# A weight load that waits for less: w_down of the first expert asked for at the gather's issue

## The chip, the cores and the metric

The kernel runs on one core of one Trainium2 chip. The metric is the device time of one launch in microseconds (us); times before and after are medians of several runs. Five engines work beside each other from queues of their own: TensorE (PE; its weight loads are PEld), VectorE (DVE), ScalarE (ACT), GpSimd (POOL) and SyncE (SP), which here only issues transfers. "SPq" and "POOLq" are the sequencers of SyncE and GpSimd. The transfers of all of them run on 16 DMA engines. Engines wait for each other through semaphores.

## The reference, cut to what matters

One layer of a hybrid encoder over 512 tokens of width 1024. First come differential attention and a state-space mixer (some 830 us of the span, not touched here); then the mixture of experts around whose start the change lies; then a gated per-layer embedding and a last norm.

```
h2 = rms_norm(x)                                   # 512 x 1024
logits = h2 @ router_w + router_b                  # 32 experts
top-4 experts for each token, softmax gates
for each expert e, on the rows of h2 that chose it:
    gu = x_e @ w_up[e] + b_up[e]                   # 1024 -> 2048
    act = (clip(u) + 1) * g * sigmoid(1.702 g)
    out = act @ w_down[e] + b_down[e]              # 1024 -> 1024
x += sum over each token's four outs, by gate
x += sigmoid(rms_norm(x) @ w_ple_gate) * (p @ w_ple_proj)
y = rms_norm(x)
```

## The kernel before

Each expert is a block of 96 rows (CAP). The rows of a block are gathered from h2_dram by GpSimd (`fetch`, an indirect DMA with a list of token numbers) into the tile xg; TensorE turns them in eight transposes (`turn_x`), VectorE copies the result out of PSUM (`copy_x`, L1864), and TensorE multiplies them by w_up (`up`, 192 matmuls of 512 columns and 12 for the bias, L2017). ScalarE and VectorE make the activation, TensorE turns it (`turn_act`) and multiplies it by w_down (`down`, 144 matmuls) one round later. So a round is: `up(b)`, `turn_x(b + 1)`, `down(b - 1)`, `turn_act(b)`. In rounds 3, 7, 11, ... a block is small and takes less of TensorE. With these inputs no expert needs a second block.

The weights of an expert are 8 MB of w_up and 4 MB of w_down. The on-chip memory holds one expert's w_up, in eight tiles of 1 MB, and one expert's w_down, in four pairs of 1 MB. SyncE asks for each tile of the next expert as soon as TensorE has used that tile for the last time (`up_used`, `down_used`). All of SyncE's transfers stand in one queue of the DMA engines, q1, in the order in which they were asked for; GpSimd's gathers are in q0, ScalarE's stores in q10.

Before the first expert the order is written out by hand (L578 to L600). SyncE loads w_up of expert 0 early, then four rows of w_ple_gate, then the biases of expert 0 once the routing is chosen (L590 to L592). Then it waits until the rows of the first gather have landed (`xg_landed`, L593) and asks for w_down of expert 0 (L594, issued at L569), then for the other rows of w_ple_gate when TensorE has finished the projections (`ple_projected`, L595), then for w_up of expert 1, tile by tile as TensorE frees them (L598, issued at L555). w_down of expert 0 is wanted by TensorE only in round 1, after `up(1)`.

GpSimd waits for the table of slots (`tables_ready`) and for h2 to be stored, and issues gather 0 (`fetch(0)`). `fetch(1)` waits for its landing and for the transposes of block 0 (`x_turned`), since both gathers write xg. `gather_cleared` is incremented ahead of each gather at L741; nothing in the kernel before waits for it. VectorE, meanwhile, works on the tables for the later blocks (L1820 to L1859) and comes to `copy_x(0)` behind them.

Of the kernel before, what the change touches and what calls it, by code (L numbers as in the profile page):

```python
# [119 lines left out]
def wait(eng, sem, value):  # L120

    if not isinstance(value, int) or value > 0:
        eng.wait_ge(sem, value)
# [30 lines left out]
def build(nc, x, p, mix_norm_w, w_in, lambda_q1, lambda_k1, lambda_q2, lambda_k2, da_head_norm_w,  # L154
# [3 lines left out]
    with ExitStack() as ctx:  # L158
# [3 lines left out]
        def sem(name):  # L162
            return ctx.enter_context(nc.semaphore(name))
# [285 lines left out]
        rstd_ready, gather_cleared = sem("rstd_ready"), sem("gather_cleared")  # L449
# [35 lines left out]
        def _(sp):  # L485
# [79 lines left out]
            def load_down(i, expert):  # L565
                for c in range(KT // 2):
                    if not isinstance(i, int) or i:
                        sp.wait_ge(down_used, KT * (i - 1) + 2 * c + 2)
                    sp.dma_start(w_dn_pair[c], w_dn_d[ds(expert, 1), c].rearrange("e p a n -> (e p) a n")  # L569
                                 ).then_inc(rows_landed[c], 16)  # L570

            def load_bias_down(i, expert):
                wait(sp, down_done, i)
                for n in range(2):
                    sp.dma_start(bias_dn[32 * n:32 * n + 3, 0:D - 512 * n],  # L575
                                 bdn_dram[:, ds(expert * D + n * 512, D - 512 * n)]).then_inc(bias_dn_landed, 16)
# [13 lines left out]
            sp.wait_ge(chosen_ready, TT)  # L590
            load_bias_up(0, 0)
            load_bias_down(0, 0)  # L592
            sp.wait_ge(xg_landed, 16)  # L593
            load_down(0, 0)  # L594
            sp.wait_ge(ple_projected, 2 * TT)  # L595
            for k in range(4, KT):
# [61 lines left out]
        def _(pool):  # L658
# [69 lines left out]
            def fetch(b, column=None):  # L728

                wait(pool, xg_landed, 16 * b)  # L730
                if isinstance(b, int) and b < 2:
                    wait(pool, x_turned, b)
                    token = slot_token[:, b:b + 1]
                else:
                    if column is None:
                        column = pool.value_load(control[0:1, ds(b, 1)], min_val=0, max_val=BLOCKS - 1)
                    pool.tensor_copy(block_token[:], slot_token[:, ds(column, 1)]).then_inc(block_token_ready, 1)
                    pool.wait_ge(block_token_ready, b - 1)
                    wait(pool, x_turned, b)
                    token = block_token[:]  # L740
                pool.sem_inc(gather_cleared, 1)  # L741
                pool.indirect_dma_start(xg, None, h2_dram, bass.IndirectOffsetOnAxis(token, 0), bounds_check=SEQ - 1,  # L742
                                        oob_is_err=False).then_inc(xg_landed, 16)

            def experts_again():
                with pool.Fori(EXPERTS, ROUNDS) as b:
                    fetch(b, pool.value_load(control[0:1, ds(b + AGAIN, 1)], min_val=0, max_val=BLOCKS - 1))

            pool.wait_ge(tables_ready, 1)
            for b in range(2):  # L750
                pool.wait_ge(h2_stored[b], 16 * TT // 2)
            fetch(0)
            fetch(1)
            pool.wait_ge(tables_ready, 3)
            with pool.Fori(2, EXPERTS) as b:
# [1912 lines left out]
```

## Time and profile before

| what | us |
|---|---|
| median of 3 runs | 1959.93 (1958.43 to 1961.11) |
| the profiled execution | 1959.75 |
| its span in the trace | 1958.0 |
| TensorE busy in the span | 1889.7 (97%) |
| VectorE / ScalarE / GpSimd busy | 709.3 / 482.6 / 101.8 |
| DMA, mean over the span | 261 GB/s, 511.92 MB |

Times in the rows are microseconds from the start of the span unless marked ns. In windows, each engine's busy time stands with its number of instructions, then PEclk, the clock of TensorE that was granted as a share of full speed, the busy share of the 16 DMA engines, and GB/s. The share comes out slightly over 1 when they are all busy. In a row of a line, the durations are min/median/max in ns, and then come the first and last start. In a row of a queue stand packets, MB and the share of the 16 engines' time. A row of landing gives the time from a transfer's issue until its semaphore said that it was complete, min/median/max.

### The profile page before, as it was taken

The page shows a single profiled execution, that of the slowest core. Times are in us where ns is not written, and L with a number is a line of the kernel's source. Part 1 is how long each engine was busy: PE and PEld are TensorE (multiplying, and loading weights), DVE is VectorE, ACT ScalarE, POOL GpSimd, SP SyncE. Part 2 cuts the span into 40 slices and gives each one's busy share as a digit, 9 for nine tenths or more (in the row PEclk, how much of TensorE's full clock was granted, in tenths as well). Part 3 has the DMA queues.
Part 4 walks back from the last instruction along what each step waited for, and adds up shares of the span by engine and source line. Part 5 has one row for each costly group of instructions (what it writes and reads, how often), then busy time and mean ns, then how long its engine had stood idle before and what let it go on. Part 6 is the DMA issues. An engine that isn't in the chain of part 4 may idle for free.

```text
span 1958.0 us, 37027 instructions
## 1 busy us (share of the span) xinstructions
PE 1889.7 (97%) x15105; PEld 1115.0 (57%) x15105; DVE 709.3 (36%) x1104; ACT 482.6 (25%) x736; POOL 101.8 (5%) x137
## 2 busy tenths in 40 slices
PE   6999999999999999989999999999999999999998
PEld 4777788888888888833434334343333343433346
DVE  5666768887865445261001010010100000101056
ACT  3444443535435333211000110001010000010135
POOL 2000001001020000000000000000000000000030
PEclk8999999999999999999999999999999999999999
DMA  4333322222222543299999999999999999999962
GB/s 129 88 89 106 85 76 65 67 73 64 65 64 66 150 117 98 102 377 415 407 415 417 415 415 414 414 412 412 410 414 411 408 413 414 407 411 405 408 243 94
DMA packets 206279, 511.92 MB, mean 261 GB/s; under 512 B 16341, under 2 KB 127558, under 8 KB 173382
## 3 DMA queue, kind: packets, MB, share of 16 engines
q1 hardware_dynamic: 189296, 474.68, 63.3%
q10 hardware_dynamic: 9942, 18.50, 2.8%
q0 software_dynamic: 6912, 16.79, 2.4%
q8 instruction: 110, 1.80, 0.4%
q14 instruction: 19, 0.16, 0.0%
HBM read 497.79 MB, written 20.51 MB: 265 GB/s over the span
## 4 chain that ended last, share of the span: by engine, by line
PE 69%; SPq 15%; DMA 7%; DVE 4%; issue 2%; ACT 2%; ACTq 0%; POOL 0%; DVEq 0%
PE psum L2017 65%; SPq L569 7%; DMA arena<-bup_dram 7%; SPq L555 3%; SPq L562 3%; SPq L575 2%; PE psum L2408 1%; PE psum L2416 1%; DVE arena L1436 1%; SPq L603 0%; PE psum L2079 0%; DMA arena<-y_dram,rows_u 0%; PE psum L2187 0%; PE psum L2147 0%; ACT w_hi L816 0%
## 5 line engine op out<-in xcount | busy, mean ns | idle before, releaser
L2017 PE MATMUL psum<-arena 128*32 128x512 f32 (+5 forms) x10352 | 1054.3, 529 | 30.8 <-DMA arena<-in_w_up 9.3
L2017 PEld LDWEIGHTS psum<-arena 128*32 128x32 f32 (+2 forms) x10352 | 434.0, 115 | 604.3 <-issue 423.2
L1870 DVE TENSOR_SCALAR arena<-psum 128x768 f32<-128x768 f32 (+1 forms) x32 | 28.8, 899 | 921.2 <-ACT arena L1141 921.2
L2017 PE MATMUL psum<-h_hi,w_hi 128*128 128x512 f32 x640 | 258.7, 404 | 1.3 <-DVE w_lo L1320 1.3
L2017 PE MATMUL psum<-h_hi,w_lo 128*128 128x512 f32 x640 | 249.9, 390 | 0.0
L2017 PE MATMUL psum<-h_lo,w_hi 128*128 128x512 f32 x640 | 249.4, 390 | 0.0
L1320 DVE TENSOR_TENSOR w_lo<-arena,w_hi 128x1024 fp32r<-128x1024 f32 x104 | 135.7, 1305 | 187.5 <-ACT w_hi L816 186.6
L1141 ACT ACTIVATE arena<-psum 128x768 f32<-128x768 f32 (+1 forms) x32 | 24.5, 764 | 570.5 <-PE psum L2017 570.5
L2017 PEld LDWEIGHTS psum<-h_hi,w_hi 128*128 128x128 f32 x640 | 120.3, 188 | 34.5 <-issue 8.8
L2017 PEld LDWEIGHTS psum<-h_lo,w_hi 128*128 128x128 f32 x640 | 120.4, 188 | 26.4 <-issue 2.9
L2017 PEld LDWEIGHTS psum<-h_hi,w_lo 128*128 128x128 f32 x640 | 120.1, 188 | 25.8
L816 ACT ACTIVATE w_hi<-arena 128x1024 fp32r<-128x1024 f32 x104 | 109.6, 1055 | 96.1 <-PE psum L2017 96.1
L1167 ACT ACTIVATE arena<-psum 128x768 f32<-128x768 f32 (+1 forms) x32 | 24.5, 764 | 336.6 <-PE psum L2416 336.6
L742 POOL DMA_INDIRECT arena<-h_dram,block_token x30 | 30.7, 1022 | 657.0 <-PE psum L2408 657.0
L890 ACT ACTIVATE arena<-psum 128x512 f32<-128x512 f32 x40 | 23.8, 596 | 149.6 <-PE psum L2017 149.5
L708 POOL TENSOR_TENSOR arena<-after,gdta 128x1024 f32<-128x1024 f32 x16 | 33.0, 2064 | 511.0 <-DVE gdta L1519 371.0
L1504 DVE SCALAR_TENSOR_TENSOR arena<-arena,gconv 128x512 f32<-128x512 f32 x72 | 54.2, 752 | 2.6
L2017 PE MATMUL psum<-ys_hi,w_hi 128*128 128x512 f32 x128 | 49.8, 389 | 0.0
L2017 PE MATMUL psum<-ys_lo,w_hi 128*128 128x512 f32 x128 | 49.8, 389 | 0.0
L2017 PE MATMUL psum<-ys_hi,w_lo 128*128 128x512 f32 x128 | 49.8, 389 | 0.0
L870 ACT ACTIVATE arena<-arena,small 128x128 f32<-128x128 f32 (+3 forms) x64 | 35.5, 555 | 31.1 <-DVE small L1442 31.1
L2017 PEld LDWEIGHTS psum<-arena,ones_bf 32*32 32x32 bf16 (+1 forms) x609 | 8.2, 88 | 45.3 <-issue 43.4
(381 smaller groups left out, 1627.8 us busy)
## 6 DMA issues: line engine op xcount, KB each, us to landing
arena<-in_w_up SPq DMA_DIRECT2D x256, 1024.0 KB, 18.7
arena<-in_w_down SPq DMA_DIRECT2D x128, 1024.0 KB, 22.7
arena<-in_w_in SPq DMA_DIRECT2D x80, 512.0 KB, 3.9
arena<-in_w_ssd_branch SPq DMA_DIRECT2D x16, 512.0 KB, 4.1
y_dram<-arena ACTq DMA_DIRECT2D x24, 288.0 KB, 6.6
y_dram<-arena ACTq DMA_DIRECT2D x8, 512.0 KB, 4.0
arena<-in_w_attn_branch SPq DMA_DIRECT2D x8, 512.0 KB, 3.9
arena<-in_w_out SPq DMA_DIRECT2D x8, 512.0 KB, 4.6
```

Source lines behind the costliest of these rows:

```text
L555: sp.dma_start(w_up_part[k], w_up_d[ds(expert, 1), k].rearrange("a p n -> (a p) n")).then_inc(w_up_landed[k], 16)
L562: sp.dma_start(bias_up[32 * r:32 * r + 3, :].rearrange("q (c n) -> q c n", c=2), rows[:, r:STRIPS + 1:STRIPS - r]).then_inc(bias_up_landed ...
L569: sp.dma_start(w_dn_pair[c], w_dn_d[ds(expert, 1), c].rearrange("e p a n -> (e p) a n")).then_inc(rows_landed[c], 16)
L575: sp.dma_start(bias_dn[32 * n:32 * n + 3, 0:D - 512 * n], bdn_dram[:, ds(expert * D + n * 512, D - 512 * n)]).then_inc(bias_dn_landed, 16)
L708: pool.tensor_tensor(dta_after, after[:].unsqueeze(1).broadcast_to([P, HG, P]), gdta[:, c, :].unsqueeze(2).broadcast_to([P, HG, P]), ALU.m ...
L742: pool.indirect_dma_start(xg, None, h2_dram, bass.IndirectOffsetOnAxis(token, 0), bounds_check=SEQ - 1, oob_is_err=False).then_inc(xg_land ...
L816: act.activation(w_hi[:, unit.slot], w_raw[unit.slot], ACT.Copy).then_inc(hi_ready, 1)
L870: ins = act.activation(s, s, ACT.Exp, bias=amax[:, 2 * q + m:2 * q + m + 1], accum_out=asum[:, 2 * q + m:2 * q + m + 1])
L1320: dve.tensor_tensor(w_lo[:, unit.slot], w_raw[unit.slot], w_hi[:, unit.slot].bitcast(F32), ALU.subtract).then_inc(lo_ready, 1)
L1504: ins = dve.scalar_tensor_tensor(out=o, in0=r[:, k:k + SEQ], scalar=gconv[:, k, i:i + 1], in1=o, op0=ALU.mult, op1=ALU.add)
L1870: dve.tensor_scalar(u_sb[:, 0:n], up_psum[:, 0:n, 1, :], 1.0 + LIMIT, 1.0 - LIMIT, ALU.min, ALU.max).then_inc(u_ready, 1)
L2017: return pe.matmul(o, l, r, start=start, stop=stop)
```

## The change

SyncE's wait ahead of the first w_down is for `gather_cleared` at 2 instead of `xg_landed` at 16. `gather_cleared` reaches 1 ahead of the first gather, as before, and 2 by a new increment that GpSimd executes behind it, in block 0 alone. Nothing else is changed; the gather still lands in xg, TensorE still waits for `xg_landed`.

```
@@ block.sync
             load_bias_up(0, 0)
             load_bias_down(0, 0)
-            sp.wait_ge(xg_landed, 16)
+            sp.wait_ge(gather_cleared, 2)
             load_down(0, 0)
             sp.wait_ge(ple_projected, 2 * TT)
@@ block.gpsimd, fetch(b)
                 pool.sem_inc(gather_cleared, 1)
                 pool.indirect_dma_start(xg, None, h2_dram, bass.IndirectOffsetOnAxis(token, 0), bounds_check=SEQ - 1,
                                         oob_is_err=False).then_inc(xg_landed, 16)
+                if isinstance(b, int) and b == 0:
+                    pool.sem_inc(gather_cleared, 1)
```

## Rows read from the trace of the kernel before

**Rows 1.** The page: busy time, GB/s in 40 slices, chain by engine

```profile
PE 1889.7 (97%) x15105; PEld 1115.0 (57%) x15105; DVE 709.3 (36%) x1104; ACT 482.6 (25%) x736; POOL 101.8 (5%) x137
...
GB/s 129 88 89 106 85 76 65 67 73 64 65 64 66 150 117 98 102 377 415 407 415 417 415 415 414 414 412 412 410 414 411 408 413 414 407 411 405 408 243 94
...
PE 69%; SPq 15%; DMA 7%; DVE 4%; issue 2%; ACT 2%; ACTq 0%; POOL 0%; DVEq 0%
```

**Rows 2.** Two long windows; columns: stretch, length, busy by engine, PEclk, DMA share, GB/s

```profile
860.00:1240.00 380.00, 377.32 (x4031) 151.08 (x4035) 38.67 (x58) 34.36 (x46) 14.64 (x25) 1.00 1.02 414
1240.00:1840.00 600.00, 581.11 (x6153) 227.86 (x6149) 48.93 (x57) 51.54 (x68) 21.50 (x35) 1.00 1.01 411
```

**Rows 3.** TensorE's largest wait for a transfer after 960 (us in total, times, longest)

```profile
PE psum L2017 <- DMA arena<-in_w_up: 9.3, 13, 1.2
```

**Rows 4.** Windows around the first gather, columns as in rows 2

```profile
854.00:859.00 5.00, 3.15 (x12) 1.30 (x11) 3.79 (x17) 1.20 (x3) 0.87 (x2) 0.90 0.51 121
857.00:858.00 1.00, 0.87 (x8) 0.69 (x8) 0.83 (x6) 0.00 (x0) 0.00 (x0) 1.00 0.00 0
```

**Rows 5.** Timelines of SP, POOL, PE and DVE, 840 to 910 (start, length, both us)

```profile
856.98 2.13 SPq L569 DMA_DIRECT2D arena<-in_w_down  x4
859.16 2.02 SPq L597 DMA_DIRECT2D pg_raw<-in_w_ple_gate  x4
...
853.45 1.24 POOL L742 DMA_INDIRECT arena<-h_dram,slot_token  x1 [72.81 <-DVE control L1828]
...
851.89 4.38 PE L2017 MATMUL psum<-w_pp,p_turned_at 128*128 128x512 f32 x6
857.09 0.87 PE L2408 MATMUL psum<-ident,arena 96*128 96x96 f32 x8 [0.81 <-DMA arena<-h_dram,slot_token]
860.14 20.81 PE L2017 MATMUL psum<-arena 128*32 128x512 f32 x192 [2.19 <-DVE arena L1864]
...
885.08 0.94 PE L2416 MATMUL psum<-ident,arena 128*128 128x128 f32 x6 [2.53 <-DVE arena L1878]
885.95 22.38 PE L2017 MATMUL psum<-arena 128*32 128x512 f32 x192
...
859.13 0.96 DVE L1864 COPY arena<-psum 128x768 f32<-128x768 f32 x1 [0.97 <-DVE rows_u L1859]
```

**Rows 6.** GpSimd at the third gather: its sequencer (POOLq) and the gather, by line

```profile
L742 POOLq MOVE  x1: 38/38/38, 882.2 to 882.2; - x1
L742 POOL DMA_INDIRECT arena<-h_dram,block_token x1: 1025/1025/1025, 883.0 to 883.0; - x1
...
L755 POOLq ALU_OP  x1: 38/38/38, 882.8 to 882.8; - x1
```

**Rows 7.** Gathers to landing: first, second, other 30; queues in 860:863, in 863:865

```profile
DMA to landing us min/median/max: 3.5/3.5/3.5
...
DMA to landing us min/median/max: 8.0/8.0/8.0
...
DMA to landing us min/median/max: 7.1/8.6/9.5
...
q1 hardware_dynamic: 321, 1.25, 102.1%
...
q0 software_dynamic: 123, 0.31, 40.0%
```

**Rows 8.** Window in TensorE's second expert, matmuls and weight loads alone, PEclk, DMA share, GB/s

```profile
886.00:890.60 4.60, 4.60 (x32) 1.12 (x36) 0.65 1.03 419
```

**Rows 9.** Requests of 1 MB issued at 857.0, 890.5, 946.0, to landing; gather queue in 948:950

```profile
DMA to landing us min/median/max: 4.9/4.9/4.9
...
DMA to landing us min/median/max: 9.2/9.2/9.2
...
DMA to landing us min/median/max: 7.6/7.6/7.6
...
q0 software_dynamic: 105, 0.18, 24.6%
```

More of the change, by code:

```diff
@@ L592, in _ @@
             load_bias_down(0, 0)
-            sp.wait_ge(xg_landed, 16)
+            sp.wait_ge(gather_cleared, 2)
             load_down(0, 0)
@@ L743, in fetch @@
                                         oob_is_err=False).then_inc(xg_landed, 16)
+                if isinstance(b, int) and b == 0:
+                    pool.sem_inc(gather_cleared, 1)
             def experts_again():
```

## The prediction

> **What bounds the kernel now.** I read the page first. TensorE is busy 97% of the span, and the chain that ended last is 69% TensorE, 15% SyncE's issuing and 7% transfers. The GB/s row is between 64 and 150 in the first 17 slices and above 400 in almost all of the expert stage [rows 1]. So that stage may be bound by transfers, by TensorE, or by each in turn. Two long windows tell which: from 860 to 1240 and from 1240 to 1840 the DMA engines have no idle time (share 1.02 and 1.01, 414 and 411 GB/s), and TensorE is idle for 2.7 us of the first 380 and 18.9 us of the next 600 [rows 2]. The 2.7 us is a wait for VectorE of 2.53 [rows 5]; later it waits for transfers, the weights of w_up above all (9.3 us in 13 waits) [rows 3]. So TensorE catches up with a stream of transfers that never pauses, and the place of the last bytes in that stream sets the end.
>
> From this follows the accounting. A transfer asked for earlier helps if the stream had a hole that it fills, and if no later hole opens for it. A later TensorE hurts only if it frees a weight buffer so late that the stream runs dry.
>
> There is a hole. From 854 to 859 the traffic is 121 GB/s on the mean, with none at 857 [rows 4]. The timelines around it [rows 5]: GpSimd's first gather is recorded at 853.45 for 1.24 us. SyncE asks for w_down at 856.98, when that gather has landed. TensorE turns the gathered rows at 857.09 to 857.96, VectorE, busy with the routing tables until then, copies them at 859.13, and TensorE starts the first expert at 860.14.
>
> **The change, step by step.**
>
> *When SyncE wakes.* The new increment stands behind the gather in GpSimd's program. It fires either when the sequencer comes to it or when the list is written. Behind the third gather the sequencer starts the loop's next instruction at 882.8, while the gather is recorded at 883.0 and lasts 1.02 us more: it doesn't wait for the list [rows 6]. By this spacing the increment comes 0.2 us ahead of the first gather's record, at about 853.2; if it waits for the list, at 853.45 + 1.24 = 854.7. The request for w_down moves forward from 856.98 by 3.8 us, or else by 2.3. I take the first.
>
> The Trainium skill (Perfetto Trace Analysis, DMA Instruction — SWDGE and Sequencer-only Instruction) has the sequencer ready for its next instruction as soon as the gather is pushed into the wait queue, and an instruction of the sequencer alone executed there. This agrees with the row of the third gather, and speaks against the change: the wait would then hold w_down back for nothing that the gather has done.
>
> *SyncE's queue behind it.* The four w_down requests take 2.13 us of issuing. The four rows of w_ple_gate behind them wait for TensorE's projections, which end at 851.89 + 4.38 = 856.3, so they issue from 856.3 instead of 859.16 [rows 5]. The next request, w_up of expert 1, waits for TensorE's first freed buffer and follows TensorE. On GpSimd's queue the second gather waits for the first one's rows and their transposes; it moves with them, and is wanted only after the first expert, 21 us on.
>
> *What the gather pays.* Before, the stream was running out as the first gather was issued, and it landed in 3.5 us. The second, issued among the requests for w_down and w_ple_gate, took 8.0; the other 30 took 7.1 to 9.5 [rows 7]. With w_down asked for at 853.2, the first is in the place of the second: requests of 1 MB are in the queue when its list is complete. I take 8.0, which is 4.5 us later. Bounds: 3.6 (7.1), 6.0 (9.5), and 0 if its packets still go first (rival 1). The transposes then end at 857.96 + 4.5 = 862.5.
>
> Some of this is hidden. VectorE takes the turned rows at 859.13 whatever comes before, 1.1 us after it could have had them (857.96 and the 0.1 of a hand-over). So TensorE's first expert starts 4.5 − 1.1 = 3.4 us later, near 863.5 (bounds 2.5 to 4.9). All of TensorE up to 1240 follows, since it waits for no transfer there [rows 2].
>
> *How two queues share.* From 860 to 863, 1.2 to 4.2 us into the second gather, the only queue of the DMA engines at work is SyncE's, q1, at 102.1%; from 863 to 865 the gather's queue q0 has 40% of their time for 0.31 MB [rows 7]. So the sharing itself is mild, and most of the price is that the gather's first packets move late. The Trainium skill (DMA: Bandwidth & Descriptors, Queues, rings and completion order) says that each DMA engine takes turns between its queues, packet by packet. The row of 863 to 865 agrees; by that rule alone the gather would lose only about the time of its own bytes, and the change would end as rival 1 does. The row of 860 to 863 is against it.
>
> *The clock.* After the idle of 2.53 us before 885.08, the granted clock of 886 to 890.6 is 0.65, a mixture of TensorE's two levels of 1.2 and 2.4 GHz, and the 192 matmuls there take 22.38 us against 20.81 in the first expert [rows 5, 8]. Now TensorE is to do only 0.87 us of transposes from 856.3 to 863.5. The price is between 0 and 22.38 − 20.81 = 1.6 us; I take the middle, 0.8. TensorE is then 3.4 + 0.8 = 4.2 us late.
>
> *What a late TensorE costs.* How near the stream is to running dry can be read from the weight requests, which SyncE makes when TensorE frees a buffer. Into the empty queue at 857.0 a request of 1 MB landed in 4.9 us. At 890.5 it took 9.2 us, and the shortest in that stretch, at 946.0, took 7.6 [rows 9]; so the stream had at most 7.6 − 4.9 = 2.7 us of earlier work before it. Part of this isn't cover but sharing with the gather of that time, which moved 0.18 MB in 948 to 950 and a little before; 0.3 MB at 414 GB/s is 0.7 us. I take 2.0 us of cover, near the upper bound since only the gather speaks against that; bounds 2.7, and 0 if all of the difference is sharing and late completion.
>
> *The sum.* A stream that runs dry at 946 starts again at TensorE's pace, and what was gained at 855 comes out there as a hole. So the end moves by TensorE's delay less the cover: 4.5 − 1.1 + 0.8 − 2.0 = +2.2 us. With the cheap bounds of all it is 3.6 − 1.1 + 0 − 2.7 = −0.2, with the dear ones 6.0 − 1.1 + 1.6 − 0 = +6.5. The profiled execution took 1959.75 us around its span of 1958.0, the median of the three runs is 1959.93; I put the shift on the median: 1962.1. Costed at nothing: the increment itself, on a sequencer that then waits for the landing anyway, and VectorE's work behind the copy, which moves 3.4 us and isn't wanted during the 20.81 us of the first expert.
>
> **The rivals.**
>
> *1. The gather isn't slowed*, because the increment waits for the list or the gather's packets move ahead of w_down's. For it: the gather would have a start of about a microsecond, and the sharing is mild. Against: all 31 gathers in a busy stream took 7.1 us or more. TensorE then keeps its times, and the stream moves forward by no more than the cover at 946: −2.0 us, 1957.9 (1957.2 with 2.7, 1960 with none).
>
> *2. No cover at 946* (the other side, slower by over 0.2%). The 7.6 us there are sharing and late completion, and nothing is queued when the request comes. For it: it is the shortest landing of the stage. Against: the DMA share has no gap, here or anywhere [rows 2]. The whole delay of 4.2 us comes out: 1964.1. It decides from a cover below 0.3 us.
>
> *3. The full hole is gained.* TensorE's delay never empties the stream, as it catches up by 1240 anyhow. The five microseconds lack 5 × (414 − 121) / 414 = 3.5 us of traffic; the gather's late bytes need some of it, so some 3 us are gained: 1956.9. Against: the shortness of the 7.6.
>
> **How the numbers follow.** Forecast 0.50, rival 1 0.22, rival 2 0.18, rival 3 0.10. What a measurement of this kernel can tell from no change is about 0.2%, 3.9 us. The forecast's own range is 1960 to 1965.5, of which I put 0.07 above +3.9 us; of rival 2, whose price is 0.3 above that bound, 0.12. Below −3.9 us lie 0.03 of rival 3 and 0.02 of rival 1. So slower 0.19, faster 0.05, the same 0.76. The range that leaves out no more than 0.2 goes from the low end of rival 1 to the forecast's upper end: 1957.2 to 1965.5.
>
> **What would show it.** SyncE's w_down request at 853.2 (854.7 by the other reading). No microsecond without traffic at 855 to 859. The first gather landing in 8.0 us, TensorE's first expert at 863.5, perhaps with a lower clock behind it. A DMA share below 1 near 950. From then on the same pace as before, everything 2 us later. The prediction is wrong if the first gather lands in under 5 us, if no hole opens near 950, or if TensorE's delay leaves no trace at the end.

## The result

The changed kernel takes 1965.05 us (median of 10, 1963.99 to 1967.12), the kernel before 1959.74 us (median of 10, 1958.43 to 1961.69): the ratio is 1.0027 with a 95% interval of 1.0018 to 1.0036, so +5.3 us, slower by over 0.2%. The forecast was 1962.1 in a range of 1957.2 to 1965.5. Its mechanism holds in the main: the gather is slowed, TensorE is late, and the stream of transfers runs dry for it. The hole came at another place than forecast, and the price was under-estimated by 3 us.

The profiled execution took 1965.11 us around a span of 1963.4. Times of two executions are compared from the start of the first gather's record: 853.45 before [rows 5], 852.27 now. Nothing ahead of it was changed in any kernel here, and yet it starts between 851.83 and 854.13 in the 13 profiled executions. First come the timelines of the changed kernel that answer to [rows 5] (start, length):

Timeline, the changed kernel:

```profile
852.06 2.12 SPq L569 DMA_DIRECT2D arena<-in_w_down  x4
855.14 1.82 SPq L597 DMA_DIRECT2D pg_raw<-in_w_ple_gate  x4
...
852.27 1.24 POOL L742 DMA_INDIRECT arena<-h_dram,slot_token  x1 [72.81 <-DVE control L1830]
...
860.43 1.54 PE L2410 MATMUL psum<-ident,arena 96*128 96x96 f32 x8 [5.33 <-DMA arena<-h_dram,slot_token]
863.02 23.03 PE L2019 MATMUL psum<-arena 128*32 128x512 f32 x192 [1.05 <-DVE arena L1866]
...
890.18 0.87 PE L2418 MATMUL psum<-ident,arena 128*128 128x128 f32 x6 [2.53 <-DVE arena L1880]
890.99 22.50 PE L2019 MATMUL psum<-arena 128*32 128x512 f32 x192
...
862.01 0.96 DVE L1866 COPY arena<-psum 128x768 f32<-128x768 f32 x1 [5.04 <-PE psum L2410]
```

By line, the changed kernel:

```profile
L745 POOLq EVENT_SEMAPHORE  x1: 17/17/17, 852.0 to 852.0; - x1
```

The new increment (L745) runs at 852.0, ahead of the gather's record at 852.27 that it stands behind in the program, and SyncE's w_down request follows at 852.06. So it was the sequencer's, as forecast; the request comes 0.2 us before the gather's record instead of 3.5 us after it. TensorE gets the rows at 860.43 after 5.33 us of waiting, runs the transposes in 1.54 us instead of 0.87, and begins the first expert at 863.02: 10.75 us after the gather's record, where it was 6.69. From the gather's record to the end of the span it is 1963.4 − 852.27 = 1111.1 us, where it was 1958.0 − 853.45 = 1104.6.

How the gather landed, and the queues up to its first packets (853.5 to 856.75) and from there (856.75 to 860), answering to [rows 7]:

By line, the changed kernel:

```profile
DMA to landing us min/median/max: 8.1/8.1/8.1
```

DMA queues, the changed kernel:

```profile
q1 hardware_dynamic: 302, 1.17, 89.8%
...
q1 hardware_dynamic: 285, 1.10, 82.7%
q0 software_dynamic: 144, 0.25, 20.1%
```

The gather lands in 8.1 us instead of 3.5. Its list is complete at 852.27 + 1.24 = 853.5, and for 3.2 us the only queue that moves anything is SyncE's; the gather's 0.25 MB come after 856.75, among w_down's. In the kernel before its first packets moved at 855.3, some 0.6 us after its list was complete at 854.7. So 2.6 of the 4.6 us are a later start, and the other 2.0 us come while the two queues share the engines. The windows that answer to [rows 2, 4] follow, with 858 to 859 (TensorE waits), 863 to 867 (the first expert), 890 to 900 and 950 to 960 added:

Windows, the changed kernel:

```profile
854.00:859.00 5.00, 1.11 (x3) 0.19 (x1) 2.77 (x12) 1.81 (x2) 0.00 (x0) 0.83 1.02 414
858.00:859.00 1.00, 0.00 (x0) 0.00 (x0) 0.00 (x0) 1.00 (x1) 0.00 (x0) 0.50 1.00 406
863.00:867.00 4.00, 3.98 (x20) 0.97 (x24) 3.93 (x18) 0.00 (x0) 0.84 (x1) 0.50 1.04 412
890.00:900.00 10.00, 9.82 (x74) 3.23 (x78) 0.13 (x1) 0.81 (x1) 0.18 (x1) 0.83 0.51 181
950.00:960.00 10.00, 10.00 (x144) 6.21 (x137) 1.08 (x2) 0.13 (x1) 0.24 (x2) 1.00 1.00 377
1240.00:1840.00 600.00, 581.51 (x6142) 227.44 (x6138) 46.52 (x55) 51.52 (x68) 21.55 (x35) 1.00 1.01 411
```

The hole at 854 to 859 is gone: 414 GB/s instead of 121. The clock is at 0.50, the lower level of 1.2 GHz, from 858 on, while TensorE waits, and the first expert runs at it until past 867. The hole comes back at 890 to 900, where the DMA engines are busy for 0.51 of the time at 181 GB/s: half of ten microseconds is lost where 3.5 were gained. Near 950, where it was forecast, there is none (the share is 1.01 in 940 to 950 and 1.00 in 950 to 960). From 1240 the stream is as full as before (1.01, 411 GB/s), so nothing makes up for it.

The Trainium skill (Perfetto Trace Analysis, Sequencer-only Instruction) says that the profiled window of such an instruction is its execution by the sequencer; L745's 17 ns at 852.0, before the gather's record has begun, agree with that.

### The profile page after: what moved, and what is told of

Read it like the earlier page. It is cut to its first block, busy times and chain, and to the rows that moved or that the text cites. A ratio compares the mean times of both kernels' runs of the same rounds, so it can differ in the third digit from the quotient of the medians.

```text
span 1963.4 us, 37028 instructions
## 1 busy us (share of the span) xinstructions
PE 1892.6 (96%) x15105; PEld 1117.9 (57%) x15105; DVE 709.3 (36%) x1104; ACT 482.6 (25%) x736; POOL 103.1 (5%) x137
## 4 chain that ended last, share of the span: by engine, by line
PE 70%; SPq 12%; DMA 11%; DVE 4%; issue 2%; ACT 2%; ACTq 0%; DVEq 0%; POOLq 0%
PE psum L2019 66%; DMA arena<-bup_dram 10%; SPq L569 5%; SPq L555 3%; SPq L562 2%; SPq L575 1%; PE psum L2410 1%; DVE arena L1438 1%; PE psum L2418 1%; PE psum L2081 0%; DMA arena<-h_dram,slot_token 0%; PE psum L2189 0%; SPq L603 0%; PE psum L2149 0%; ACT w_hi L818 0%
```

## The experiments

Theory A: the gather pays for the w_down requests that are queued when its list is complete; TensorE's lateness, with a share for its clock, empties the stream later on; the filled hole is worth nothing by itself. Rivals: B, any w_down beside the gather slows it; and, of the end, that w_down's early transfers cost something by themselves.

In the table, "TensorE" is the start of the third expert's w_up product counted from the first gather's record, in the profiled execution, against 921.06 − 853.45 = 67.61 us of the kernel before (line below). The end is the ratio to the kernel before, run on the same chip. Each median is of 8 to 11 runs.

The third expert, the kernel before and the changed kernel:

```profile
921.06 9.22 PE L2017 MATMUL psum<-arena 128*32 128x512 f32 x84
...
926.23 4.07 PE L2019 MATMUL psum<-arena 128*32 128x512 f32 x36
```

| kernel | gather lands | TensorE, us against before | median, us | ratio (95% interval) |
|---|---|---|---|---|
| changed kernel | 8.1 | +6.4 | 1965.05 | 1.0027 (1.0018 to 1.0036) |
| changed kernel again | 8.0 | +6.1 | 1965.44 | 1.0027 (1.0016 to 1.0037) |
| 1: request behind the written list | 3.6 | 0.0 | 1959.99 | 1.0001 (0.9992 to 1.0010) |
| 2: 1 MB of w_down early | 5.3 | +3.1 | 1962.29 | 1.0018 (1.0009 to 1.0027) |
| 3: request 3 us later than before | 3.6 | +0.1 | 1962.04 | 1.0014 (1.0005 to 1.0023) |
| 4: TensorE held back | 3.6 | +6.2 | 1963.78 | 1.0021 (1.0012 to 1.0030) |
| 5: change, TensorE kept busy | 8.0 | +2.0 | 1960.53 | 1.0006 (0.9997 to 1.0016) |
| 6: before, second wait filled | 3.6 | +1.2 | 1960.00 | 1.0003 (0.9994 to 1.0012) |
| 7: 1 and 6 together | 3.6 | −1.7 | 1957.15 | 0.9990 (0.9981 to 0.9999) |
| 8: before, both waits filled | 3.7 | −0.4 | 1960.01 | 1.0003 (0.9994 to 1.0012) |
| 9: 1 and 8 together | 3.6 | −1.7 | 1957.59 | 0.9985 (0.9976 to 0.9994) |
| 1 again | 3.6 | 0.0 | 1959.76 | 0.9999 (0.9989 to 1.0008) |

The profiled executions also have an end of their own, counted from the gather's record to the end of the span, against the 1104.6 us of before: +6.6 and +6.1 in the changed kernel, +5.4 in experiment 4, +2.6 in 2, +2.3 in 5, +3.1 in 3, −0.7 and −0.2 in 1. So TensorE's lateness comes out nearly whole where it is late. Single executions are rough: experiments 7 and 9, both 1.7 us early, are at −3.1 and −0.8.

**1. The increment behind the written list.**

```
-                    pool.sem_inc(gather_cleared, 1)
+                    own.then(pool.memset(block_token[:], 0))
+                    pool.sem_inc(gather_cleared, 1)
```

> The changed kernel with the increment moved behind the list: GpSimd writes zeros into block_token after the gather (its engine takes instructions in order), waits for that, and only then increments. Theory A, the gather pays for the w_down requests that are queued when its list is complete: the request now comes some 1.5 to 2 us after the gather's record begins, behind its packets; the gather lands in 3.5 to 4.5 us as before, TensorE's first expert starts 6.7 us after the gather's record as before, and the transfers' hole is shorter by about 2 us. Theory B, the gather pays for any w_down that runs beside it: it lands in 7 us or more and TensorE starts 3 us late as in the changed kernel. Of the end: if the time before the expert stage's request at 946 is tight on both sides (no cover), A gives 0 to -0.5 us against the kernel before; if a filled hole counts in full, -2 us; B gives +3 to +5 us.

GpSimd's and SyncE's timelines of this kernel:

Timeline, experiment 1:

```profile
853.68 1.24 POOL L742 DMA_INDIRECT arena<-h_dram,slot_token  x1 [72.84 <-DVE control L1831]
854.93 0.11 POOL L745 MEMSET block_token<- 128x1 uint32 x1
...
855.12 2.15 SPq L569 DMA_DIRECT2D arena<-in_w_down  x4
```

Windows, experiment 1:

```profile
854.00:859.00 5.00, 3.36 (x13) 1.53 (x11) 3.99 (x19) 1.19 (x2) 1.03 (x2) 0.88 0.75 260
```

The memset at 854.93 ends behind the list (853.68 + 1.24 = 854.92), the request goes out at 855.12, 1.44 us after the gather's record began, and the gather lands in 3.6 us; TensorE is untouched. A holds and B falls. The hole at 854 to 859 is half filled (260 GB/s instead of 121), (260 − 121) × 5 / 414 = 1.7 us of transfers earlier, and the end does not move. How long that lead lasts shows in the landings of later requests. Before, at 912.4 and 924.1:

By line, the kernel before:

```profile
DMA to landing us min/median/max: 8.4/8.4/8.4
...
DMA to landing us min/median/max: 7.9/7.9/7.9
```

By line, experiment 1, the same two requests and the one of 946:

```profile
L569 SPq DMA_DIRECT2D arena<-in_w_down x1: 405/405/405, 912.6 to 912.6; - x1
DMA to landing us min/median/max: 6.5/6.5/6.5
...
L555 SPq DMA_DIRECT2D arena<-in_w_up x1: 371/371/371, 924.3 to 924.3; - x1
DMA to landing us min/median/max: 7.7/7.7/7.7
...
L569 SPq DMA_DIRECT2D arena<-in_w_down x1: 411/411/411, 946.2 to 946.2; - x1
DMA to landing us min/median/max: 6.9/6.9/6.9
```

By line, experiment 3:

```profile
L569 SPq DMA_DIRECT2D arena<-in_w_down x1: 412/412/412, 946.0 to 946.0; - x1
...
DMA to landing us min/median/max: 10.4/10.4/10.4
```

The requests come as long after the gather's record as before, but at 912.6 the transfer lands 1.9 us sooner, and at 924.3 only 0.2 us. So nearly all of the lead is lost between these two, 20 us and more ahead of the 946 that the prediction took for the tightest place. At 946 the first request lands in 6.9 us instead of 7.6 [rows 9], but the next one in 7.8 instead of 7.5: no lead is left there that these landings could show.

**2. One pair early, three behind the landing.**

```
             sp.wait_ge(gather_cleared, 2)
-            load_down(0, 0)
+            load_down(0, 0, 0, 1)
+            sp.wait_ge(xg_landed, 16)
+            load_down(0, 0, 1)
```

> The early increment of the changed kernel, but only the first 1 MB of w_down is asked for at it; the other three wait for the gather's landing, as in the kernel before. Theory A (the gather's packets start when the bytes requested before its list are through): 1 MB is through 2.5 us after it begins to move, so the gather's first packets come near 4 us after its record begins and it lands in 5.5 to 6.5 us, not 8.1; TensorE's first expert starts 1.5 to 2.5 us later than before. Theory B (fixed price of a loaded queue): 7.5 to 8.5 us, as in the changed kernel. The end by A, with TensorE's lateness coming out in full: +1.5 to +4 us, the upper part if the clock drops on the first expert; by B +4 to +6.

By line, experiment 2:

```profile
DMA to landing us min/median/max: 5.3/5.3/5.3
```

Timeline, experiment 2:

```profile
857.87 1.54 PE L2412 MATMUL psum<-ident,arena 96*128 96x96 f32 x8 [2.62 <-DMA arena<-h_dram,slot_token]
860.46 22.63 PE L2021 MATMUL psum<-arena 128*32 128x512 f32 x192 [1.05 <-DVE arena L1868]
```

The gather lands in 5.3 us, a little under A's 5.5 to 6.5 and far from B's 7.5 to 8.5: the price goes with what is queued. The start of the first expert is 860.46 − 852.51 = 7.95 us after the gather's record, 1.3 late; the clock then adds 1.8 (22.63 us instead of 20.81). In the 1.3 us, 0.7 are the clock's as well, for the transposes take 1.54 us instead of 0.87. Here the drop of the clock costs more than the gather's delay that led to it.

**3. The request later.** The kernel before with

```
-            sp.wait_ge(xg_landed, 16)
+            sp.wait_ge(x_copied, 1)
```

> The kernel before with w_down of expert 0 asked for 3 us later, when VectorE has copied the first block's rows; TensorE's work is not touched. If the stream's place sets the end as much as TensorE's (no cover on either side), the end moves by 2.5 to 3.1 us. If TensorE's pace alone sets it, or the stream has cover to give, less than 1 us.

SyncE asks at 860.11 instead of 856.98, TensorE's work up to 1000 is where it was, and the end is 0.14% later, 2.7 us by the ratio and 2.2 by the medians. The request at 946 takes 10.4 us instead of 7.6 (line above): 2.8 us more of earlier work in front of it, which goes on to the end. So the stream's place does count, when it gets worse. With experiment 1 this says that the stream has next to nothing to give on either side: 3 us later costs 2 to 3 us, and 1.7 us earlier brings nothing.

**4. TensorE late, transfers as before.** The kernel before with

```
                 turn_x(0, 0)
+                keep_busy(66)
                 up(0)
```

and `keep_busy(n)`, n times `pe.transpose(psum[:, 4 * 512:4 * 512 + P], ident[:], ident[:])`.

> The kernel before with TensorE held back ahead of the first expert by 66 transposes of the identity into an unused bank of PSUM (they compute nothing that is used); w_down's wait stays for the gather's landing. This puts TensorE's first expert some 6 us late with transfers as before. If the loss of the changed kernel is TensorE's lateness alone and the earlier request is worth nothing, the end moves by the same amount as TensorE's second down product does, 5 to 6.3 us, with a hole of the transfers near 892 like the changed kernel's. If there is 2 to 2.7 us of cover, 3.3 to 4.3 us. If the loss came from w_down's early transfers themselves, under 1 us.

Timeline, experiment 4:

```profile
857.83 7.37 PE L2553 MATMUL psum<-ident 128*128 128x128 f32 x66
865.13 20.81 PE L2017 MATMUL psum<-arena 128*32 128x512 f32 x192
...
891.54 22.97 PE L2017 MATMUL psum<-arena 128*32 128x512 f32 x192
```

Windows, experiment 4:

```profile
895.00:900.00 5.00, 5.00 (x48) 1.43 (x44) 0.00 (x0) 0.00 (x0) 0.18 (x1) 0.91 0.57 188
```

TensorE is 6.2 us late, and a hole opens at 895 to 900 (share 0.57) although w_down was asked for where it always was. The end is 4.1 us later by the ratio (2.4 to 5.9), 3.9 by the medians, under the 5 to 6.3 expected for full payment and near the 3.3 to 4.3 of 2 us of cover; the interval holds most of both. Its runs lie in groups, 1961.3 to 1961.5, 1963.4 to 1963.8 and 1965.2 to 1966.8; the profiled one is of the last (1965.18). With the changed kernel's +5.3 for the same lateness, the interval leaves open whether the early request adds a microsecond of its own. The two profiled executions speak against it: 6.2 and 6.4 us late, they took 1965.18 and 1965.11. What is shown is that TensorE's lateness makes the hole near 895 and the larger part of the loss, without any early transfer.

**5. The changed kernel with TensorE kept busy** while it waits: `keep_busy(44)` ahead of `turn_x(0, 0)`, 8 behind it and 16 ahead of `turn_act(0)`.

> The changed kernel with TensorE kept at work where it waits: 44 transposes of the identity into an unused bank of PSUM before the gathered rows are there, 8 after their transposes and 16 before the first activation's. They compute nothing that is used. If the clock is a term of the loss of its own, the first expert's 192 matmuls take 20.8 us and not 23.0, the second's 20.8 and not 22.5, and the end comes 3 to 4.5 us before that of the changed kernel, within 2 us of the kernel before, although the gather is as slow as there. If the loss is the gather alone, less than 1 us comes back.

Timeline, experiment 5:

```profile
861.88 0.83 PE L2410 MATMUL psum<-ident,arena 96*128 96x96 f32 x8
...
863.75 20.81 PE L2019 MATMUL psum<-arena 128*32 128x512 f32 x192 [0.17 <-DVE arena L1866]
...
888.69 0.88 PE L2418 MATMUL psum<-ident,arena 128*128 128x128 f32 x6 [0.78 <-DVE arena L1880]
889.50 20.81 PE L2019 MATMUL psum<-arena 128*32 128x512 f32 x192
```

Both experts take 20.81 us, the transposes 0.83 and 0.88. The first expert starts nearly as late as in the changed kernel (863.75 − 853.40 = 10.35 us after the gather's record, there 10.75), yet TensorE is only 2.0 us late behind it, and the end is at 1960.53, 4.9 us under the changed kernel beside it (1965.44), slightly more than the 3 to 4.5 expected. But 22.50 − 20.81 = 1.7 us of this are the second expert's, which the kernel before pays too. The other 3.2 us are the clock's part of the loss, about half of it; in the changed kernel's trace it is 2.9 us (2.2 in the first expert, 0.7 in the transposes) of TensorE's 6.4. The rest is the gather's.

**The changed kernel again**, beside it:

> The changed kernel once more, beside the next three on one chip. The gather lands 8 us after its record begins and the first expert's matmuls run at half clock for a part: TensorE's second expert is behind by 6 us counted from the gather's record, the median by 4.5 to 6 us. In the first profile the part before the gather was 1.2 us shorter than in the kernel before; if that belongs to the change it shows again, if it is chance of the first loads it does not.

The part ahead of the gather was 0.4 us shorter this time, not 1.2: chance.

**6 and 7. TensorE earlier, without and with the earlier request.** `keep_busy(16)` ahead of `turn_act(0)`, in the kernel before and in experiment 1.

> The kernel before with the 16 idle-filling transposes ahead of the first activation's alone; transfers and their waits untouched. TensorE's second expert takes 20.8 us and not 22.4, so everything on it is 1.6 us earlier until 1240. If the stream's place and TensorE's pace set the end together (both tight), the end stays within 0.5 us, since the stream is where it was. If TensorE's pace alone sets it, -1.6 us.

> w_down asked for when the list is really written (the stream 2 us earlier, the gather not slowed) together with the 16 transposes (TensorE 1.6 us earlier). If both bounds are tight, so that each alone gains nothing, together they gain 1.6 to 2 us against the kernel before. If the earlier request is worth nothing at all, 0 to -0.5 us.

Timeline, experiment 6:

```profile
860.81 23.60 PE L2017 MATMUL psum<-arena 128*32 128x512 f32 x192 [2.02 <-DVE arena L1864]
...
889.35 20.81 PE L2017 MATMUL psum<-arena 128*32 128x512 f32 x192
```

Timeline, experiment 7:

```profile
860.42 20.81 PE L2020 MATMUL psum<-arena 128*32 128x512 f32 x192 [2.13 <-DVE arena L1867]
...
886.16 20.81 PE L2020 MATMUL psum<-arena 128*32 128x512 f32 x192
```

The second expert takes 20.81 us in both. But the first one, whose code and waits are those of the kernel before, took 23.60 us in the one profile and 20.81 in the other: after the same idle of 2 us it starts at half clock in some executions and not in others. So experiment 6 had no early TensorE in its profiled execution (+1.2 us), and its ratio doesn't answer its question. Experiment 7 is 2.2 us faster than before by the medians, as two tight bounds want it: TensorE 1.7 us early and the stream about 2. But TensorE alone early, which it has to be compared with, no profiled execution shows.

**8 and 9. Both waits filled**, `keep_busy(16)` behind `turn_x(0, 0)` as well, without and with the earlier request; and experiment 1 again.

> The kernel before with TensorE kept at work in both short waits, 16 unused transposes ahead of the first expert and 16 ahead of the first activation's transposes. The run with the second wait alone caught the first expert at half clock (23.60 us instead of 20.81), so that its TensorE was 1 us late instead of 1.6 early; here both experts should take 20.8 us. Transfers are where they were. With both bounds tight: end within 0.7 us of before. If TensorE's pace alone bounds: -1.6 us or more (some executions of the kernel before may pay the first drop too, and these gain 2 us more).

> The same with w_down asked for when the list is written. TensorE 1.6 us early in every execution, the stream 2 us early: -2 to -2.5 us against before, and no worse than with the second wait alone filled. If the earlier request is worth nothing, the same as the run beside it without it.

> The request at the written list alone, once more, beside the two others: 0 to -0.5 us against before if TensorE's pace is the tight bound at 946; -1.5 to -2 us if the stream's place is, as the profile of its first run in the stretch from 1300 to 1870 would have it.

Timeline, experiment 8:

```profile
857.33 3.39 PE L2553 MATMUL psum<-ident 128*128 128x128 f32 x16
860.65 20.94 PE L2017 MATMUL psum<-arena 128*32 128x512 f32 x192
```

Timeline, experiment 9:

```profile
856.27 1.91 PE L2556 MATMUL psum<-ident 128*128 128x128 f32 x16
858.51 20.81 PE L2020 MATMUL psum<-arena 128*32 128x512 f32 x192 [0.32 <-DVE arena L1867]
```

Experiment 9 confirms experiment 7: 0.9985 (0.9976 to 0.9994), some 2.5 us under the kernel before; the two are the fastest kernels here, and their intervals overlap. Experiment 8 differs from 9 in its code by the request alone and is at 1.0003. So the earlier request brings 2.4 us beside the filled waits (1957.59 against 1960.01), and nothing in the kernel as it was (experiment 1, twice). How much of the 2.4 us is the stream's isn't separated: in the profiled execution of 8 TensorE was only 0.4 us early, in that of 9 1.7. In 8 the projections had run at full clock (six matmuls in 2.82 us, 4.38 before), TensorE then waited 2.49 us for the gathered rows instead of 0.81, and the 16 transposes behind them ran mostly at half clock (3.39 us instead of 1.91). So whether an early TensorE alone gains something is not settled.

## Why the prediction was right in kind and too low by 3 us

- *The stream never pauses, and its place sets the end.* Right, together with TensorE's pace. Moved later, the stream moved the end by 2 to 3 us (experiment 3); moved earlier, it gained nothing by itself (1), and up to 2.4 us with the waits filled (8 and 9).
- *The increment fires before the list is written.* Right: 852.0 against a record of 852.27 to 853.5. With a real wait for the list nothing is lost (experiment 1).
- *The gather lands in 8.0 us instead of 3.5.* Right, 8.1; and what is queued ahead sets it: 3.6 us with the request 1.44 us behind the record, 5.3 with 1 MB early.
- *4.5 less 1.1 hidden, so 3.4 us.* 4.1 measured (10.75 − 6.69). What lacked is the transposes at half clock, 1.54 − 0.87 = 0.7 us.
- *The clock, 0.8 us, bounds 0 and 1.6.* This is the step that failed: 23.03 − 20.81 = 2.2 us in the first expert's matmuls, 2.9 with the transposes, over the upper bound. The bound was one drop's price in the second expert, which was at full clock again by 890; here TensorE had been idle for 5.33 us, was at half clock before it had anything to do, and stayed there until past 867. Experiment 5 took this part away and 4.9 us came back, with the 1.6 us that the second expert had always paid among them.
- *2.0 us of cover at 946.* Too much, and at the wrong place. In experiment 1 a lead of the stream of about 2 us was lost between 912.6 and 924.3. The comparison of 7.6 us with the 4.9 us of an empty queue took nearly all of the difference for earlier work. That it isn't is argued and not measured by itself, but in experiment 4 the first request after the hole landed in 4.9 us, but those of 901.9 to 912.1 in 6.7 to 7.1, although the stream had just been dry. Of the 2.7 us only 0.7 were put down to sharing. The changed kernel's stream ran dry in 890 to 900 already, 50 us ahead of the place forecast: the request there, which had landed in 9.2 us, now came 6.3 us later against a stream that was some 3 us earlier. What counted for the end was TensorE's lateness, 4.1 + 2.2 + 0.1 = 6.4 us, less little or nothing: +5.3 by the medians, +6.6 and +6.1 from the gather's record in the two profiled executions.
- *The sum.* 4.6 − 1.1 + 0.7 + 2.2 − 1.1 = 5.3, where the forecast had 4.5 − 1.1 + 0.8 − 2.0 = 2.2. The last 1.1 is the remainder, with an uncertainty of 1.8 from the ratio's interval, so that a cover of nothing is not excluded.
- *The signs and the chances.* One of the signs named for a wrong prediction came true: no hole opened near 950. The shift of +5.3 us is above the 3.9 us that a measurement can tell, a side to which the prediction had given 0.19. And that the time lies inside the range, 0.45 us below its end, is in part luck: the end of 1965.5 isn't the sum of the dear bounds, which is 1959.9 + 6.5 = 1966.4, and in the sum a clock above its bound is made up for by a gather that stayed 1.4 us under its own.
- *Rival 1* fell with the landing of 8.1 us; it is what experiment 1 does, without the gain of 2 us that it promised. *Rival 2*, no cover, is nearly what happened; its 1964.1 is nearer to the measured 1965.05 than the forecast. *Rival 3* fell, as the hole came back at 890 to 900.

## What to carry to other kernels

In this kernel an increment behind a DMA in the program said that the engine had been told, not that the DMA had been prepared (852.0, with the list written from 852.27 to 853.5); to order something behind it, wait for an instruction that the same engine runs after it, or for the landing. A small transfer that everything waits for should be ahead of large ones in time, by about its whole issue, since what is queued when it is ready is its price. Before a hole in the transfers is filled, look for the next place where a request waits for compute: here transfers moved earlier alone gained nothing, and together with TensorE's pace 2 to 3 us.

## What the runs showed of the hardware that I had not expected

- The same wait of 2 us of TensorE is followed by 20.81 us of matmuls in five profiled executions of kernels whose first expert starts as before, and by 23.60 in one (experiment 6). Comparisons of a microsecond need many runs where such a wait is in the path.
- Half a clock can cost more than the delay that brings it: 1.3 us of delay of the first expert brought 1.8 us of slower matmuls (experiment 2). Unused transposes in the wait, 5.01 us ahead of the gathered rows and 1.04 us behind their own, took it away (experiment 5).
- A gather's packets started 3.2 us after its list was complete, in a queue of their own, although the earliest of the w_down requests ahead of it was 1.4 us old (changed kernel). SyncE's queue moved 1.17 MB of its 4 MB in that time, so the gather did not wait for all that had been asked for ahead of it; what it did wait for stays open. Sharing by turns, as the Trainium skill has it (DMA: Bandwidth & Descriptors, Queues, rings and completion order), is seen from 856.75 on, with 20.1% of the time for the gather, and not in the 3.2 us before.
